# Four modulation vectors moved from matmuls to VectorE, and two of six products of a first half merged into one matmul, in a one-core encoder layer

## The reference

```python
mod = silu(c) @ w_ada + b_ada                 # c: one vector of 1024 for the prompt, one for the sample
sh1, sc1, g1, sh2, sc2, g2 = split(mod, 6)    # six modulation vectors of 1024
h = rmsnorm(x) * (1 + sc1) + sh1
proj = h @ w_in                               # 6152 columns: inputs of two recurrences, gates
o_hg, o_gdn = recurrences(proj)               # HGRN2 and gated DeltaNet, 4 heads of 128 each
y = sigmoid(gate_a) * (o_hg @ w_pa) + sigmoid(gate_b) * (o_gdn @ w_pb)
x = x + g1 * (y @ w_out)
h = rmsnorm(x) * (1 + sc2) + sh2
x = x + g2 * ((silu(h @ w_up_gate) * (h @ w_up)) @ w_down)     # inner width 2816
return rmsnorm(x)
```

## Time and profile before

| | us |
|---|---|
| median of 3 runs (lowest, highest) | 1006.21 (1003.43, 1006.83) |
| the profiled execution, its own time | 1004.13 |
| its span, first to last instruction | 1002.3 |
| TensorE busy | 970.5 |
| VectorE busy | 487.8 |
| ScalarE busy | 365.0 |

### The profile page before, as it was taken

The page is one execution under the profiler, slowest core; times in us unless marked ns, Lnnn a source line. Parts: engine busy times, 40 slices in busy tenths (PEclk is TensorE's granted clock), DMA queues, the critical chain, the costliest instruction groups (busy, mean ns, idle before and its releaser), DMA issues.

```text
span 1002.3 us, 23390 instructions
## 1 busy us (share of the span) xinstructions
PE 970.5 (97%) x10189; PEld 939.4 (94%) x10189; DVE 487.8 (49%) x878; ACT 365.0 (36%) x628; POOL 18.6 (2%) x29
## 2 busy tenths in 40 slices
PE   5989999999999999999999999999999999999996
PEld 5889888998999998999999999999999999999996
DVE  3569645532246356266435854444444444324242
ACT  6578345523324442563232232322222332121222
POOL 0100000000010000000000000000000000000000
PEclk9999999999999999999999999999999999999998
DMA  9822334414343535323533222222233322322312
GB/s 331 251 63 63 87 94 113 114 45 108 85 124 104 139 113 149 90 79 106 165 105 105 86 85 85 84 84 84 84 85 91 94 85 80 93 82 79 95 37 90
DMA packets 181103, 103.64 MB, mean 103 GB/s; under 512 B 4530, under 2 KB 179320, under 8 KB 180892
## 3 DMA queue, kind: packets, MB, share of 16 engines
q1 hardware_dynamic: 179484, 96.01, 34.0%
q0 software_dynamic: 912, 4.17, 1.2%
q10 hardware_dynamic: 624, 2.23, 0.6%
HBM read 99.07 MB, written 3.31 MB: 102 GB/s over the span
## 4 chain that ended last, share of the span: by engine, by line
PE 91%; DVE 3%; ACT 3%; issue 2%; DMA 0%; ACTq 0%; DVEq 0%
PE G L1764 76%; PE R L1772 12%; PE R L1775 2%; PE G L1809 1%; DVE w_lo L1280 1%; ACT w_hi L954 0%; DMA xtok<-in_x_prompt 0%; DVE cy L1442 0%; DVE cy L1441 0%; ACT L931 0%; DVE relT L1488 0%; ACT L970 0%; ACT inp L970 0%; ACT rn L982 0%; DVE cy L1438 0%
## 5 line engine op out<-in xcount | busy, mean ns | idle before, releaser
L1764 PE MATMUL G<-h_hi,w_hi 128*128 128x272 f32 (+1 forms) x1456 | 431.1, 296 | 4.6 <-DVE w_lo L1280 3.3
L1764 PE MATMUL G<-h_lo,w_hi 128*128 128x272 f32 (+1 forms) x1456 | 421.3, 289 | 0.0
L1764 PE MATMUL G<-h_hi,w_lo 128*128 128x272 f32 (+1 forms) x1456 | 420.8, 289 | 0.0
L1764 PEld LDWEIGHTS G<-h_hi,w_hi 128*128 128x128 f32 x1456 | 275.5, 189 | 8.7 <-issue 4.4
L1764 PEld LDWEIGHTS G<-h_lo,w_hi 128*128 128x128 f32 x1456 | 275.8, 189 | 0.0
L1764 PEld LDWEIGHTS G<-h_hi,w_lo 128*128 128x128 f32 x1456 | 275.5, 189 | 0.0
L1280 DVE TENSOR_TENSOR w_lo<-raw,w_hi 128x1024 fp32r<-128x1024 f32 (+2 forms) x138 | 158.4, 1148 | 223.2 <-ACT w_hi L954 222.8
L954 ACT ACTIVATE w_hi<-raw 128x1024 fp32r<-128x1024 f32 (+2 forms) x138 | 136.3, 988 | 98.7 <-PE G L1764 89.7
L1764 PE MATMUL G<-a_hi,w_hi 128*128 128x272 f32 (+2 forms) x340 | 98.5, 290 | 0.4 <-DVE w_lo L1280 0.4
L1764 PE MATMUL G<-a_hi,w_lo 128*128 128x272 f32 (+2 forms) x340 | 98.2, 289 | 0.0
L1764 PE MATMUL G<-a_lo,w_hi 128*128 128x272 f32 (+2 forms) x340 | 98.0, 288 | 0.0
(11 more groups left out here) (277 smaller groups left out, 1163.8 us busy)
## 6 DMA issues: line engine op xcount, KB each, us to landing
raw<-in_w_in SPq DMA_DIRECT2D x48, 512.0 KB, 5.2
raw<-in_w_up SPq DMA_DIRECT2D x44, 512.0 KB, 3.8
raw<-in_w_ada SPq DMA_DIRECT2D x32, 512.0 KB, 4.8
wada<-in_w_ada SPq DMA_DIRECT2D x8, 1024.0 KB, 11.2
raw<-in_w_down SPq DMA_DIRECT2D x16, 512.0 KB, 3.7
raw<-in_w_out SPq DMA_DIRECT2D x8, 512.0 KB, 3.7
raw<-in_w_down SPq DMA_DIRECT2D x8, 384.0 KB, 3.3
xT<-in_x_t POOLq DMA_DIRECT2D x1, 2176.0 KB, 9.8
```

What stands on the lines that cost most here:

```text
L1764: ins = pe.matmul(out, w, x, start=(job.first and k == 0 and p == 0), stop=(job.last and k == job.nk - 1 and p == 2))
```

## The change

**Modulation.** The 16 `ada` groups, their copies and the four `ada_mod` steps go. The weights `w_ada` of the four vectors are laid out by output on the host (`w_ada_t`: 64 *units* of 128 outputs x 512 inputs). GpSimd's queue loads them into two buffers, unit u+2 when unit u is used. `silu(c)` of the prompt and of the sample is broadcast to all partitions (`c_part`, loaded in two halves over the same queue, silu on ScalarE: `c_half`, `c_silu`). One `ada_part` is one VectorE instruction that multiplies 512 weights by `c_part` and sums them into a column of `mod` (first half of the inputs) or of `mod_half`, which lies in `c_cols` (second half). There are 128 of them, and the table `BETWEEN` says before which step how many stand. `ada_sum` adds the halves and the bias, before `gain2`, which moves from behind `pa` 0 to behind `pa` 7.

**Products.** In the groups of `MERGED` the first half becomes columns 0 to 255 and the second 256 to 543 (545 where two shift columns ride along). High and low activations lie in one tile (`o_both`, ...), so that one matmul of 512 columns makes `w_hi*x_lo` and `w_hi*x_hi` side by side in one bank; `w_lo*x_hi` (256 columns) is added to the first. The second half keeps its three products, now of 288 columns. Before a group can be read, ScalarE copies 256 columns from the bank to `sq` (`copy_part`), and VectorE adds them to the other 256 in PSUM (`join_slot`): 76 copies and 76 adds.

```diff
+    (('g_y', 1, 4), 4), (('g_y', 1, 5), 4), ...     # BETWEEN: before this step, so many ada_part steps
...
-    weave(gdn_steps(0, ahead), parts_of(*braid([gk1, gq0, gq1, gv0, gv1, *hg_inputs("hf", 0)], ada_parts(5)), fine=True))
+    weave(gdn_steps(0, ahead), parts_of(gk1, gq0, gq1, gv0, gv1, *hg_inputs("hf", 0), fine=True))
...
+    n = 0
+    for before, count in BETWEEN:
+        at = next(i for i, x in enumerate(plan) if key(x) == before)
+        for _ in range(count):
+            plan.insert(at, ("ada_part", n // 2, n % 2))
+            at, n = at + 1, n + 1
+            if n == 2 * ADA_TILES:
+                plan.insert(at, ("c_half", 1))
...
+                if name == "ada_part" and step[2] and step[1] + 2 < 2 * ADA_TILES:
+                    pool.wait_ge(unit_used, step[1] + 1)
+                    load_unit_of_ada(step[1] + 2)
...
+            def copy_part(g):
+                ...
+                act.activation(part_of(g), G[:, g % 2, 0, 0:EDGE], ACT.Copy).then_inc(part_copied, 1)
...
+            def join_slot(g):
+
+                whole = slot_cols(g % 2, 0, EDGE)
+                dve.wait_ge(part_copied, walk.plus(merged.index(g) + 1, 4))
+                dve.tensor_tensor(whole, whole, part_of(g), ALU.add).then_inc(slot_whole, 1)
+                dve.wait_ge(slot_whole, walk.plus(merged.index(g) + 1, 4))
...
+                elif name == "ada_part":
+                    u, g = a
+                    half = u // ADA_TILES
+                    if g == 0:
+                        if u:
+                            dve.wait_ge(unit_used, u)
+                        dve.wait_ge(c_part_ready, half + 1)
+                        dve.wait_ge(unit_in[u % 2], 16 * (u // 2 + 1))
+                    to = (mod[:, 2 * KD:6 * KD, :], mod_half)[half][:, u % ADA_TILES, g:g + 1]
+                    ins = dve.scalar_tensor_tensor(acc[:, 0:HK], ada_tile(u)[:, :], 1.0, c_part[:, g, :],
+                                                   ALU.mult, ALU.mult, accum_out=to)
...
-                        for p, (w, x) in enumerate(((wh, xh), (wh, xl), (wl, xh))):
-                            ins = pe.matmul(out, w, x, start=(job.first and k == 0 and p == 0),
-                                            stop=(job.last and k == job.nk - 1 and p == 2))
+                        if half or groups[job.group][0] not in MERGED:
+                            passes = [(out, wh, xh), (out, wh, xl), (out, wl, xh)]
+                        else:
+                            passes = [(bank.rearrange("p (x t) -> p x t", x=2), wh, low_high[job.src](job.k0 + k)),
+                                      (bank[:, 0:EDGE], wl, xh)]
+                        for p, (to, w, x) in enumerate(passes):
+                            ins = pe.matmul(to, w, x, start=(job.first and k == 0 and p == 0),
+                                            stop=(job.last and k == job.nk - 1 and p == len(passes) - 1))
```

More of the change, by code:

```diff
@@ L38 @@
 TOK = SEQ + DEC
-HALF = TOK // 2
+EDGE = 2 * P
+MERGED = ("pa", "pb", "out", "ffg", "ffu", "down")
 NH = 4
@@ L136, in parts_of @@
                 job = jobs[s[1]]
[L137 to L140, removed]
+                if fine:
                     for q, ks in enumerate(THIRDS):
@@ L381, in make_plan, with key @@
             plan.insert(at, ("g_scale" if plan[n][0] == "g_norm" else "o_scale", *plan[n][1:]))
+    def key(step):
+        name = step[0]
+        if name == "evac":
+            return (name, *groups[step[1]][:2])
+        if name in ("job", "half", "more", "split_next", "split", "split_hi", "split_lo"):
+            return (name, *groups[jobs[step[1]].group][:2], *step[2:])
+        return step
+    n = 0
[6 more added lines that the diff above has]
+                plan.insert(at, ("c_half", 1))
+    assert n == 4 * ADA_TILES
+    for half, before in enumerate((("g_row", 0), ("ada_part", ADA_TILES, 0))):
+        plan.insert(plan.index(before), ("c_silu", half))
     return jobs, groups, plan
@@ L541, in build, with ada_tile @@
         o_gate_z = at("rec", "o_gate_z", [P, 2, TOK])
+        w_ada_t = [at("rec", "w_ada_t0", [P, HK], off=base + 2 * tile + 2 * (PACK + 2) * QUAD * 4 + PACK * P * 2),
+                   at("rec", "w_ada_t1", [P, HK]),
+                   at("rec", "w_ada_t2", [P, HK], off=kd_at)]
+        assert 2 * tile + 2 * (PACK + 2) * QUAD * 4 + PACK * P * 2 + HK * 4 <= KD * row
+        mod_half = c_cols[:, 0:2, :].rearrange("p a (n g) -> p (a n) g", g=2)
+        moved = next(i for i, x in enumerate(plan) if x == ("h_end", 1))
+        early_units = sum(x[0] == "ada_part" and x[2] == 0 for x in plan[:moved])
+        def ada_tile(u):
+            return w_ada_t[2 if u % 2 == 0 and u >= early_units else u % 2]
         def og_row(hd):
@@ L584, in build, with pairs, part_of @@
         src = dict(h=(h_hi, h_lo), o=(o_hi, o_lo), y=(y_hi, y_lo), h2=(h_hi, h_lo), a=(a_hi, a_lo))
+        def pairs(both, apart):
+            return lambda k: both[:, k:k + apart + 1:apart, 0:EDGE]
+        low_high = dict(o=pairs(o_both, 2 * NH), y=pairs(y_both, 28), h2=pairs(h_both, KD), a=pairs(a_both, KF))
+        merged = [g for g, x in enumerate(groups) if x[0] in MERGED]
+        def part_of(g):
+            return sq[:, 1, g % 2 * EDGE:(g % 2 + 1) * EDGE]
         G = ctx.enter_context(nc.psum_tensor("G", [P, 2, 2, 512], F32))
@@ L1752, in products @@
                         hi, lo = src[job.src]
-                        edge = SPLIT if job.group == ending else HALF
-                        cols_ = slice(edge, TOK + 2 if job.src == "h2" else TOK) if half else slice(0, edge)
-                        out = G[0:job.m, job.group % 2, half, 0:cols_.stop - cols_.start]
+                        cols_ = slice(EDGE, TOK + 2 if job.src == "h2" else TOK) if half else slice(0, EDGE)
+                        bank = G[0:job.m, job.group % 2, half, :]
+                        out = bank[:, 0:cols_.stop - EDGE] if half else bank[:, 512 - EDGE:512]
                         at = job.k0 + k
@@ L1858, in _ @@
                     fill(n, 0, [tr(lambda b: R[:, b, 0:P], ada_rows[:, a[0] % 2, :])])
-                elif name == "ada_mod":
-                    wait_slot(pe, groups_at["ada", (a[0], KD // 2 - 1)])
-                    for k in range(2):
-                        fill(n, k, [tr(lambda b, j=j: R[:, b, j * P:(j + 1) * P], ada_part[:, 4 * k + j, :])
-                                    for j in range(4)])
                 elif name == "sums":
```

228 lines of the change are left out of this document (129 added, 99 removed).

## The result

The change makes the kernel slower: 1011.62 us (median of 9 runs, 1008.75 to 1013.02) against 1006.21 (9 runs of the kernel before beside them), a ratio of 1.0049 with a 95% interval of 1.0038 to 1.0059. The forecast was 991 us. The profiled execution took 1013.02 us; against the 1004.13 of before that is +8.9, where the sum said -14.2.

The account below looks back on a forecast made before the run. It took every stage after the start as bound by TensorE at full clock. Against the profiled 1004.1 us: -20.1 - 3.9 + 4.8 + 5 = 989.9, or 992.0 against the median; forecast 991 us, range 980 to 1001.

Parts of the forecast that it names:

- (b): At the first ffg and ffu, which end together, the wait for ffg's slot grows from 0.20 to 1.1 us: +0.9.
- I take 5 us in all, bounds 0 and 14: TensorE waits caused by the moved vectors: late loads, the second half of c_part, and VectorE late by part of an instruction.
- one in 3.3 us: Densest stretch, second pair: 21 units over 70 us; loads allow one every 2.6 to 3.5 us, so 0 to 4 us late.
- Three places are not covered: Joins delay TensorE in pb/pa (3.0 us), at the first ffg/ffu (0.9) and in the last group (0.9): 4.8 us, bounds 3 and 8.
- So for 8 k this is covered: In groups of 8 k (6.0 us) the slot is free 0.9 us later but needed a whole group later, so no wait.
- Rival (2): Joins wait in every group: 0.9 us in 60 groups of out, ffg, ffu, down, +54 us, some 1040 us; chance 0.04.
- The merged product: -3.9: One 512-column matmul (232 ns) replaces two of 119.0: 6 ns for each of 656 k, 3.9 us won, bounds nothing and 8.
- rival (3): A 512-column matmul costs no more than a narrow one (133.3 ns): 69 us would go, 922 us; chance 0.02.
- Removed from TensorE: -20.1: Taking 16 ada groups (16.2 us) and 4 ada_mod steps (4.0) off TensorE gains 20.1 us before any new wait.
- (1): Rival: loads set the pace; at 6.8 us a load the gain is gone, at 8.4 about 1020 us; chance 0.07.
- (4): Rival: VectorE's lateness eats the gain, 0.4 us at each of some 40 places, 16 us: 1000 to 1009 us; chance 0.10.
- The signs that the text named: Among them: VectorE's DMA waits short in 110 to 290 us, TensorE idle no more than now from 600 to 975 us.

Follow-up runs that it names:

- no_parts: The whole change without the 128 VectorE instructions, their loads and silu of the broadcast vector, so the four vectors are only the bias; 993.58 us, ratio 0.9873.
- table_only: The whole change with only the table replaced: 51 places, one or two whole units at each; 993.67 us, ratio 0.9873.
- pause: The kernel before, with three added TensorE pauses in front of out 2, 4 and 6, each waiting for six GpSimd memsets; 1022.69 us, ratio 1.0172.
- warm: The change without merged product, plus 14 unused matmuls of 512 columns where TensorE idles waiting for Um; 1000.34 us, ratio 0.9947.
- hi_ahead: The whole change, but in ffg/ffu ScalarE makes the next w_hi right behind its copy, ahead of silu and a_hi; 1005.86 us, ratio 1.0010.
- ada_only: The change with the four vectors moved to VectorE but no merged product, copies or adds; 1003.41 us, ratio 0.9961.
- merge_only: The kernel before with the merged product, copies and adds alone, the four vectors staying on TensorE; 1013.85 us, ratio 1.0074.
- lo_first: The change with the 51-place table, w_hi ahead of silu and a_hi in ffg/ffu, and pa's next w_lo ahead of join, ya and val; 985.23 us, ratio 0.9801.
- spread: The change without merged product and with a new table of 51 places, one or two whole units at each; 984.65 us, ratio 0.9795.

## Why the prediction was wrong

By stages, with the terms of its sum sorted into them: up to the first `ya` -13.2 (three of four `ada_mod`, the groups, +5, one join of 0.9), measured +4.0. `pa`/`pb` +1.6, measured +3.5. From there to the first `g_act` -0.4, measured -0.1. `ffg`/`ffu` -1.2 (the merged product -2.1, the wait (b), which lies behind the first `g_act`, +0.9), measured +2.6. The end -1.1, measured -1.1. Two stages hold 21.0 of the 23.1 us, and another 1.9 are in `pa`/`pb`.

**"I take 5 us in all, bounds 0 and 14" (the moved vectors).** It was 21.2 (first `ya` 457.2 against 436.0 in `no_parts`). Its prices were not too low: 0.73 us an instruction against 0.75 to 0.95, a load 3.0 us at the median and 5.4 at most against 3.7 to 5.3. The step that failed is the rate. The working spread 21 units evenly over 70 us, "one in 3.3 us", and found nothing or 4 us late; but a load can start only when its buffer's last unit is used, so what counts is, unit by unit, the time from the last use of its buffer to the place where it is wanted. The second order listing ahead of the prediction shows such bursts, and the text there read them as "one or two whole units" while the working went on with the mean. The unit used at 146.82 was wanted at 142.50, 1.2 us after its load was issued, and a load needs 2.7 us at least. That TensorE would wait behind a late unit was right, as was the warning on the second half of `c_part`, which cost VectorE 4.1 us ahead of 294.51 and TensorE 1.5 behind it. `table_only` shows that this was the table, and not the move: with the same instructions and loads 19.3 us of the 21.2 are gone.

**The missing term.** The sum has no line for the clock, although gave it as 1.00 and the text said that new waits were to be expected. Of the 19.3 us, TensorE's waits from 110 us to the first `ya` (18.1 in the change, 6.4 in `table_only`) are 11.7. The rest fits the clock: 20 us more at 1.2 GHz, at 1.8 us for each 3.4, less what falls into the idle stretches themselves. `pause` shows that an added idle stretch brings the period with it, and the profile of `warm` that filling one takes it away; how the 19.3 divide was only worked out.

**"Three places are not covered" (the joins).** They were sized well (VectorE's added work was 33 us, at 0.43 us an add; the working took 0.42 for the chain and 0.47 for the sum): behind `pa` 0 to 3 0.84, 0.82, 0.81 and 1.01 more than before (forecast 0.7, 0.7, 0.7, 0.9), at the first `ffg` 1.1 of wait (1.1). The whole of `pa`/`pb` came out 1.9 us above its terms all the same; 0.5 of that are these waits, and what the rest is no run shows. "So for 8 k this is covered" was the step that failed. It compared the joins with the return of the slot, a whole group later, and not with the chain that was tightest: reading the group, silu or `a_hi`, `w_hi`, `w_lo`, next weight load. That chain had 0.95 us of margin in every second group, and copy and add took all of it. Rival (2) had waits in every group and priced them at 0.9 us a group, against "a chain of about 3 us now", which no row of `ffg`/`ffu` stood behind; they cost 0.1 to 0.2 us in every second group, 3.9 in all. This needed no run: rows like 627.47 and 629.64 stood in the trace before.

**The merged product: -3.9.** The step of a k was right: two steps of 0.117 us become one of 0.231 (the working had 0.119 and 0.232), and rival (3) is out by it. Where `w_lo` has its margin (`hi_ahead` against `ada_only`), the stages show 1.9 us of 2.1 in `ffg`/`ffu`, once the 0.9 of (b) is taken off, and 1.2 of 1.1 behind them.

**Removed from TensorE: -20.1.** Right within 1 us (`no_parts`).

**The rivals.** (1) set its limit, 19 us lost, at loads of 6.8 us and a steady rate; at this table loads of 3.0 us at the median cost 15.0. (4) had 40 small waits; it was a handful of 1 to 4 us, and their clock. The signs that the text named were read in the profile as it said, but two of them misled: VectorE's waits "named DMA short" hold 21.5 us in 12 waits, which is 0.3 us a unit, and TensorE's idle time from 600 to 975 us did not grow beyond the forecast while 3.9 us were lost there; the rows of the weight loads would have shown it.

## What to carry to other kernels

Work moved into another engine's idle time is priced place by place: for each piece, when its data can first be asked for, what is queued behind it, and who waits for that. A mean rate hides the one place that costs 4 us; places chosen from a trace without the work, in whole units of a buffer, were worth 18 to 19 us here. Expect behind an idle stretch of some 2 us and more of a TensorE-bound kernel a half-speed period, and add what it costs: 1.8 us measured here for one of 3.4 us, an estimated 3.4 for one of 6.8. And before an instruction is added to a chain that closes once per group, read that chain's margin from the trace, from the end of the last producer to the start of the group, since the matmul rows book a late weight load as busy: TensorE's busy share stayed at 99.6% from 600 to 985 us. The Trainium skill (Perfetto Trace Analysis, Identifying the Most-Contended Engine) warns that matmul busy time is a poor measure of how near a kernel is to its limit, because pipelined instructions look smaller in a trace, and sends the reader to the weight loads; here their rows did show the wait, 1.8 us in 9 pieces.

## What the runs showed of the hardware

From 30 us on and up to the last 12 us of the span, the periods at 1.2 GHz lasted 3.4 or 6.8 us, in one case 10.2. Each began in or shortly behind an idle stretch of TensorE, of 1.9 to 4.2 us in most cases, but also of 0.9 to 1.8 us (at 77.7 us in the change behind 0.9; 966.3 us in `no_parts` behind 1.2; 405.3 us in `warm` behind 1.7). The same stretch need not bring the same period: in the thirteen profiles 29 of 31 idle stretches of 1.9 us and more had one, the 3.1 us before about 61 us had 3.4 us behind them in most kernels, 6.8 in `merge_only`, `pause` and `lo_first`, and none in `table_only`. The price is half of the period's length less what falls into the idle time itself (1.8 us for 3.4 in `pause`).

With these periods go the differences between executions of one kernel: of the kernel before, 24 runs beside the first experiments took 1003.3 to 1015.6 us, the fastest at a mean clock of 0.993 and the slowest at 0.981, and 23 runs beside the second 1002.1 to 1010.0; `spread` took 983.7 to 986.2 in 5. A difference of two or three microseconds between two profiles of this kernel is read stage by stage, or not at all.
